# Recurrences of two mixers: chunks taken in pairs, lower grams moved ahead, no products with the zero state, filler products before the first merges

## What is computed

```python
lower = jnp.where(strict, jnp.einsum('bhncd,bhnsd->bhncs', kb, k) * decay, 0.0)
rhs = jnp.concatenate([v * beta[..., None], kb * jnp.exp(g)[..., None]], axis=-1)
sol = lax.linalg.triangular_solve(jnp.eye(C) + lower, rhs, left_side=True, lower=True, unit_diagonal=True)
...
def step(S, inp):
    qc, kc, uc, wc, gc, ac = inp
    v_new = uc - jnp.einsum('bhck,bhkv->bhcv', wc, S)
    o = jnp.einsum('bhck,bhkv->bhcv', qc * jnp.exp(gc)[..., None], S) + jnp.einsum('bhcs,bhsv->bhcv', ac, v_new)
    S = S * jnp.exp(g_last)[..., None, None] + jnp.einsum(...)
    return S, o
```

## Time and profile before

| | us |
|---|---|
| timed runs: median (lowest to highest, 3 runs) | 3484.34 (3483.23 to 3485.39) |
| profiled execution, its own time | 3478.72 |
| its span, first to last instruction | 3476.9 |
| TensorE busy | 3358.7 |
| recurrences' core, layer 0: 649.34 to 753.96 | 104.62 |
| recurrences' core, layer 1: 1802.64 to 1906.95 | 104.31 |

### The profile page before, as it was taken

The page is one execution under the profiler, slowest core; times in us unless marked ns, Lnnn a source line. Parts: engine busy times, 40 slices in busy tenths (PEclk is TensorE's granted clock), DMA queues, the critical chain, the costliest instruction groups (busy, mean ns, idle before and its releaser), DMA issues.

```text
span 3476.9 us, 47334 instructions
## 1 busy us (share of the span) xinstructions
PE 3358.7 (97%) x16932; PEld 2760.2 (79%) x16932; DVE 1424.3 (41%) x2739; ACT 1267.1 (36%) x1976; POOL 1675.9 (48%) x2052
## 2 busy tenths in 40 slices
PE   7999998899999999999989999999899999999999
PEld 6888776788888888887668888878667888888887
DVE  5431598855221322148786522123663110441100
ACT  4222436534222322234563422232533332433321
POOL 6765542006665566655400466645304555435554
PEclk9999999799999999999979999999999999999999
DMA  5443321003443344333100344332102222212222
GB/s 186 145 145 109 109 91 56 13 19 133 145 144 110 127 145 145 121 103 98 61 25 1 109 145 145 127 104 82 58 1 91 97 97 97 85 61 97 97 97 97
DMA packets 104225, 340.51 MB, mean 98 GB/s; under 512 B 12144, under 2 KB 17936, under 8 KB 103968
## 3 DMA queue, kind: packets, MB, share of 16 engines
q1 hardware_dynamic: 87824, 283.08, 24.6%
q10 hardware_dynamic: 16272, 55.65, 4.8%
HBM read 330.78 MB, written 2.65 MB: 96 GB/s over the span
## 4 chain that ended last, share of the span: by engine, by line
issue 38%; POOL 33%; PE 27%; DVE 1%; POOLq 0%; ACT 0%; DVEq 0%
POOL w_lo L721 33%; PE ps L2313 7%; PE ps L2314 7%; PE ps L2315 7%; PE ps L3094 1%; PE ps L2336 0%; PE ps L3073 0%; PE ps L2337 0%; PE ps L2341 0%; PE ps L3082 0%; PE ps L3184 0%; DVE stat L2214 0%; DVE sq L2207 0%; PE ps L3190 0%; PE ps L3074 0%
## 5 line engine op out<-in xcount | busy, mean ns | idle before, releaser
L721 POOL TENSOR_TENSOR w_lo<-w_raw,w_hi 128x256 fp32r<-128x256 f32 x2040 | 1669.2, 850 | 1783.3 <-ACT w_hi L764 1776.1
L2313 PE MATMUL ps<-h_hi,w_hi 128*128 128x512 f32 x2608 | 1019.9, 391 | 0.9 <-ACT mem L981 0.9
L2315 PE MATMUL ps<-h_hi,w_lo 128*128 128x512 f32 x2608 | 1015.7, 389 | 0.0
L2314 PE MATMUL ps<-h_lo,w_hi 128*128 128x512 f32 x2608 | 1015.6, 389 | 0.0
L764 ACT ACTIVATE w_hi<-w_raw 128x1024 fp32r<-128x1024 f32 x510 | 538.2, 1057 | 927.2 <-DMA w_raw<-in_tiles 927.0
L2313 PEld LDWEIGHTS ps<-h_hi,w_hi 128*128 128x128 f32 x2608 | 490.0, 188 | 113.3 <-issue 6.4
L2315 PEld LDWEIGHTS ps<-h_hi,w_lo 128*128 128x128 f32 x2608 | 490.0, 188 | 102.9
L2314 PEld LDWEIGHTS ps<-h_lo,w_hi 128*128 128x128 f32 x2608 | 490.0, 188 | 100.3
L2314 PE MATMUL ps<-a_lo,w_hi 128*128 (+1 forms) x1120 | 435.8, 389 | 0.0
L2313 PE MATMUL ps<-a_hi,w_hi 128*128 (+1 forms) x1056 | 410.8, 389 | 0.0
L2315 PE MATMUL ps<-a_hi,w_lo 128*128 (+1 forms) x1056 | 410.8, 389 | 0.0
(11 more groups left out here) (477 smaller groups left out, 3589.4 us busy)
## 6 DMA issues: line engine op xcount, KB each, us to landing
w_raw<-in_tiles SPq DMA_DIRECT2D x510, 512.0 KB, 3.3
ada_raw<-in_ada_tiles ACTq DMA_DIRECT2D x96, 512.0 KB, 3.3
mem<-mem SPq DMA_DIRECT2D x80, 64.0 KB, 2.1
x<-in_x_t SPq DMA_DIRECT2D x2, 1024.0 KB, 6.6
sq<-in_cond ACTq DMA_DIRECT2D x4, 512.0 KB, 4.2
mem<-gates SPq DMA_DIRECT2D x8, 256.0 KB, 3.9
consts<-in_consts SPq DMA_DIRECT2D x1, 1280.0 KB, 12.8
core_mem<-gates SPq DMA_DIRECT2D x8, 128.0 KB, 2.9
```

The lines of the kernel that those rows point to most:

```text
L721: ins = nc.gpsimd.tensor_tensor(w_lo[:, s, part], w_raw[:, s, part], w_hi[:, s, part].bitcast(F32), ALU.subtract)
L2313: nc.tensor.matmul(bank, wh, hi, start=first, stop=False, skip_group_check=True)
L2314: nc.tensor.matmul(bank, wh, lo, start=False, stop=False, skip_group_check=True)
L2315: return nc.tensor.matmul(bank, wl, hi, start=False, stop=last, skip_group_check=True)
```

## The change

- The chunks are taken in two pairs, (0, 1) and (2, 3). VectorE substitutes both chunks of a pair at once (16 heads in one operation where there were 8), and the mask of the small blocks is multiplied once per pair. The merge levels alternate between the even and the odd chunk; then the even chunk, then the odd one, is run through right sides, writes and outputs.
- Level 4 masks its first product on VectorE (`mask_products`, 64 columns a head) instead of masking the lower matrix beforehand (`lower_corners`, removed), makes one product instead of two, and VectorE transposes the merged inverse (blocks of 32) for the other. ScalarE's copy of level 4 goes.
- All lower grams are made early: chunk 1 after the first turn, chunk 2 after the sixth, chunk 3 after the last, each behind a wait for PSUM to be taken. Their units are separate.
- The first chunk leaves out the products with the zero state, and `next_state(1)` writes without the old state. The state has two slots in turn.
- Eight products of 128 columns with no use stand ahead of the first level-4 products.
- ScalarE takes the decays of chunks 2 and 3 after the turns instead of before them; the silu of the gate moves there too. Output grams lie in other units, outputs in one PSUM bank.
- The constants sel_pair, sel_head and the level mask are no longer loaded.

The diff, cut to its core (ScalarE, then VectorE, then TensorE):

```diff
-                act.wait_ge(S["spread_taken"], 3 * l + 3)
-                decays(2)
-                decays(3).then_inc(S["eg_ready"], 1)
-                load_silu()
-                act.wait_ge(S["rwkv_ready"], l + 1)
-                nc.scalar.activation(mem[:, 37:39, :], core_mem[:, G_CONV + 4:G_CONV + 6, :], ACT.Silu).then_inc(S["conv_act_v"], 1)
                 for u in (2, 3, 4, 5, 0, 1):
                     turn_out(mem[:, u, :])
                 for c, u in enumerate((45, 6)):
                     turn_out_scaled(mem[:, u, :], c, ST_DELTA)
+                load_silu()
+                act.wait_ge(S["rwkv_ready"], l + 1)
+                nc.scalar.activation(mem[:, 37:39, :], core_mem[:, G_CONV + 4:G_CONV + 6, :], ACT.Silu).then_inc(S["conv_act_v"], 1)
+                nc.scalar.activation(mem[:, U_Z:U_Z + 2, :], mem[:, U_Z:U_Z + 2, :], ACT.Silu)
                 for c, u in enumerate((26, 19)):
                     turn_out_scaled(mem[:, u, :], c, ST_BETA)
-                spread_diagonal(l, 0)
-                for n in range(TB + 1):
-                    core_step(l, n)
+                act.wait_ge(S["spread_taken"], 3 * l + 3)
+                decays(2)
+                decays(3).then_inc(S["eg_ready"], 1)
+                core(l)
...
+                def mask_products(n):
+
+                    own_pair = ODD_QUARTER.unsqueeze(1).unsqueeze(3).to_broadcast([P, 4, 4, 16])
+                    for g in range(2):
+                        dve.wait_ge(S["t1_ready"], merge_turn(TB * l + n, 4, g) + 1)
+                        out, src = (ap.rearrange("p (h q c) -> p h q c", h=4, q=4) for ap in (t1_of(n, g), ps[:, merge_bank(n, g), 0:HALF]))
+                        V.tensor_tensor(out, src, own_pair, ALU.mult).then_inc(S["t1_out"], 1)
+
+                def merge16(n):
+
+                    for g in range(2):
+                        inv, inv_t = inv_units(n)[:, g, :], inv_t_units(n)[:, g, :]
+                        dve.wait_ge(S["dx_ready"], merge_turn(TB * l + n, 4, g) + 1)
+                        link(V.tensor_tensor(evens(inv, 4), evens(inv, 4), compact(ps[:, merge_bank(n, g), half[0]], 4), ALU.add))
+                        V.transpose(inv_t, inv).then_inc(S["merged16"], 1)
...
+                substitute(range(15, 0, -1))
+                dve.wait_ge(S["turned"], 10 * (l + 1))
+                dve.wait_ge(S["vf_moved"], 16)
+                spread_inverses(l, 0)
+                fresh_rows()
+                mask_products(0)
+                dve.wait_ge(S["eg_ready"], 4 * l + 4)
+                take_grams(l, 2)
+                mask_products(1)
+                take_grams(l, 3)
+                merge16(0)
+                merge16(1)
+                small_blocks(l, 2)
+                small_blocks(l, 3)
+                later = slice(P, T)
+                V.tensor_tensor(mem[:, 37:39, later], mem[:, U_QG:U_QG + 2, later], mem[:, 41:43, later], ALU.mult)
+                V.scalar_tensor_tensor(mem[:, 24:26, later], mem[:, 39:41, later], -1.0, mem[:, 41:43, later], ALU.mult, ALU.mult).then_inc(S["gdn_ready"], 1)
+                dve.wait_ge(S["gdn_ready"], l + 1)
+                take_a_grams(0, range(4))
+                substitute(range(15, 8, -1))
+                next_state(1)
+                take_a_grams(1, range(4))
+                substitute(range(8, 4, -1))
+                next_state(2)
+                substitute(range(4, 0, -1))
+                spread_inverses(l, 2)
+                mask_products(2)
+                mask_products(3)
+                merge16(2)
+                take_a_grams(2, range(4))
+                merge16(3)
+                take_a_grams(3, (0, 1))
+                next_state(3)
+                take_a_grams(3, (2, 3))
...
+                    if at == 1:
+                        pe.wait_ge(S["gram_taken"], 2 * TB * l + 2)
+                        lower_grams(l, 1)
+                    if at == 6:
+                        pe.wait_ge(S["gram_taken"], 2 * TB * l + 4)
+                        lower_grams(l, 2)
...
+                def inverse_products(n, lev):
+
+                    b = TB * l + n
...
+                    for g in range(2):
+                        pe.wait_ge(S["t1_out"], merge_turn(b, lev, g) + 1)
+                        bank = merge_bank(n, g)
+                        inv_t = lambda h: inv_t_units(n)[:, g, blk(h)]
+                        t1 = lambda h: t1_of(n, g)[:, HD * h:HD * h + HD]
+                        if lev < 6:
+                            first = 0 if lev == 4 else 32
+                            for h in range(4):
+                                ins = nc.tensor.matmul(ps[0:P - first, bank, HD * h:HD * h + HD], inv_t(h)[:, first:P], t1(h), start=True, stop=True)
+                        if lev > 4:
+                            for h in range(4):
+                                out = compact(ps[0:HD, bank, HALF + HD * h:HALF + HD * h + HD], lev)
+                                ins = nc.tensor.matmul(out, t1(h), odds(inv_t(h), lev), start=True, stop=True)
+                        ins.then_inc(S["dx_ready"], 1)
...
+                pe.wait_ge(S["turned_out"], seen["turn"])
+                lower_grams(l, 3)
+                for _ in range(8):
+                    nc.tensor.matmul(ps[:, 5, 0:P], const("ident"), const("ones"), start=True, stop=True)
+                for even in (0, 2):
+                    odd, n = even + 1, even + 1
+                    if even:
+                        pe.wait_ge(S["a_gram_out"], 4 * (TB * l + 2))
+                    lower_products(even, 4)
+                    lower_products(odd, 4)
+                    inverse_products(even, 4)
+                    inverse_products(odd, 4)
+                    if even:
+                        pe.wait_ge(S["s_out"], (TB - 1) * l + 2)
+                        pe.wait_ge(S["y_out"], TB * l + even)
+                    else:
+                        pe.wait_ge(S["gram_taken"], 2 * TB * (l + 1))
+                    a_grams(even, (0, 1))
+                    lower_products(even, 5)
+                    lower_products(odd, 5)
+                    inverse_products(even, 5)
+                    inverse_products(odd, 5)
+                    lower_products(even, 6)
+                    inverse_products(even, 6)
+                    right_sides(n)
+                    lower_products(odd, 6)
+                    writes(n)
+                    a_grams(odd, (0,))
+                    inverse_products(odd, 6)
+                    state_products(n)
+                    outputs(n)
+                    pe.wait_ge(S["merged64"], 2 * (TB * l + odd) + 2)
+                    a_grams(odd, (1,))
+                    right_sides(n + 1)
+                    writes(n + 1)
+                    state_products(n + 1)
+                    outputs(n + 1)
```

More of the change, by code:

```diff
@@ L598, in _ @@
         def _(sp):
-            first, last = 2 * P, CONST_AT["eps"]
+            first, last, small = 2 * P, CONST_AT["sel_pair"], CONST_AT["eps"]
             half = KD // 2
@@ new lines, in core @@
+                for even in (0, 2):
+                    odd, n = even + 1, even + 1
+                    spread_diagonal(l, even)
+                    spread_diagonal(l, odd)
+                    products_out(even, 5)
+                    products_out(odd, 5)
+                    merge32(even)
+                    merge32(odd)
+                    products_out(even, 6)
+                    merge64(even)
+                    right_out(n)
+                    products_out(odd, 6)
+                    writes_out(n)
+                    merge64(odd)
+                    outputs_out(n)
+                    if n + 1 == TB:
+                        for k in range(4):
+                            nc.scalar.activation(attended_hi[:, k, :], mem[:, U_Y + k, :], ACT.Copy).then_inc(S["h_hi_ready"], 1)
+                    right_out(n + 1)
+                    writes_out(n + 1)
+                    outputs_out(n + 1)
@@ L2703, in recurrences @@
                     turn(src, turn_bank(n))
-                pe.wait_ge(S["turned_out"], seen["turn"])
-                for n in range(TB + 1):
-                    core_step(l, n)
+                core(l)
                 post(l)
@@ L2790, in a_grams, with right_sides @@
+                def a_grams(n, kinds):
+                    for kind in kinds:
+                        pairs = ((kt, ap), (kt, rt)) if kind == 0 else ((nb, rt), (kg, qg))
+                        grams([a_banks(n, 2 * kind + hh) for hh in range(2)], "a_gram_ready", pairs, n)
+                def right_sides(n):
+                    b, last = TB * l + n, n - 1
+                    pe.wait_ge(S["merged64"], 2 * b)
+                    pe.wait_ge(S["a_gram_out"], 4 * b if n == 1 else 4 * b - 2)
                     if n > 1:
-                        grams((6, 7), "a_gram_ready", ((nb, rt), (kg, qg)), last)
@@ new lines, in outputs @@
+                def outputs(n):
+                    b, last = TB * l + n, n - 1
```

(7 more changed lines are left out.)

391 lines of the change are left out of this document (147 added, 244 removed).

## The result

| | before | after |
|---|---|---|
| median of the timed runs, us | 3483.85 (3482.38 to 3486.93, 8 runs) | 3497.97 (3493.27 to 3500.58, 8 runs) |
| ratio | | 1.0034, 95% interval 1.0025 to 1.0043 |
| profiled execution, us | 3478.72 | 3500.58 |
| recurrences' core, layer 0, us | 104.62 | 103.79 |
| recurrences' core, layer 1, us | 104.31 | 106.49 |

The change makes the kernel 14.1 us slower, by the medians.

What follows compares the result with a forecast made beforehand. TensorE's queue was taken to bound the kernel. In layer 0, 654.1 + 40.7 + 6.6 + 42.9 + 8.7 = 753.0 against 753.96; with layer 1 and hand-overs, about -1 us: 3483.3, range 3466 to 3500.

Steps and rivals of the forecast that it cites:

- the clock fell twice: Stated sign that the prediction is wrong: TensorE's granted clock dropping twice; no further 0.50 was expected in the first pair.
- the doubled steps: VectorE's 15 substitution steps on two chunks at once, put at 14.8 us; costing more was a sign of being wrong.
- The first merge: Start of the first pair's level 4: 654.1 us, bounds 653.3 and 657, against 649.3 before; 4.8 us lost.
- Fillers and first pair: Eight unused products raise the clock before level 4; first pair then takes 40.7 us, level 4 of it 7.2.
- rival 4: Fillers ahead of level 4 run slow and end after operands are ready: start 657, +5 us, 3489; chance 0.12.
- Rival 3: Clock falls in the first pair, or stays low beyond the second pair's output grams: +12.7 us, 3497; chance 0.26.
- The gap: Between the pairs TensorE idles 6.6 us, waiting for VectorE's state, four substitution steps and spread, 9.1 us together.
- Rivals 1 and 2: Clock stays up across the gap: 3466, chance 0.12; or no gap between the pairs: 3453, chance 0.05.
- Level 4 of the second pair: Behind the idle time it runs at half clock, with some output grams: 8.7 us lost a layer.
- Outputs with state: Chunk outputs including the state's products, put at 2.5 us from the old kernel's durations.
- The hand-overs around writes of chunks 2 and 4: TensorE to ScalarE and back, 0.7 us each, no longer covered by other work; 0.5 us a layer added.
- The spared work: Chunk 1's products with the zero state left out: 2.1 us less TensorE work a layer.

Runs made afterwards that it cites:

- no_fillers: The changed kernel without the eight unused products ahead of the first level-4 products: 3512.46 us.
- steps_early: The changed kernel with VectorE's late substitution steps and the second pair's spread moved ahead of the two state updates: 3475.25 us.
- gap_filled: The changed kernel with 22 unused products behind chunk 2's outputs, in TensorE's idle time between the pairs: 3483.30 us.
- after_state_split: The changed kernel with the state products of chunk 2's and 4's outputs moved into the hand-overs, each group with its own PSUM bank: 3487.13 us.
- after_holes_filled: The changed kernel with three unused products in each of the two hand-overs of chunks 2 and 4: 3488.53 us.
- zero_cost_back: steps_early with eight unused products where the zero-state products were left out, four ahead of chunk 1's right sides, four ahead of its outputs: 3481.56 us.
- state_split: steps_early with the state products of chunk 2's and 4's outputs moved into the hand-overs, each group with its own PSUM bank: 3463.44 us.
- gap_half: The changed kernel with two of the four late substitution steps moved ahead of chunk 2's state update: 3491.98 us.

## Why the prediction was wrong

It said 3483.3, no change that can be told, and the kernel is 14.1 us slower; 3497.97 lies inside the range, near its upper end. Two of its own signs of being wrong came true: the clock fell twice in layer 0's core, and the doubled steps took 14.87 us for 14.8, the second without weight. Step by step:

- **The first merge** was to start 4.8 us later. It started 7.6 later (656.92 for 649.34), of which 2.56 come from the start of the kernel and 0.94 from the attention, which the change does not touch. 4.1 are left, and in layer 1 5.4, counted from the same place in the attention: right within its bounds. The substitution took 14.9 us (638.97 to 653.84).
- **Fillers and first pair** (rivals 3 and 4): level 4 at 7.2 us, in layer 0 no half clock from its first product to chunk 2, in layer 1 0.9 us of it at level 4's start. Right; no_fillers shows that the eight products are why. They ended after the operands were ready, as rival 4 says, but by 0.9 and 1.5 us and inside the bounds of the start. Rival 3's time, 3497, is met by chance: its mechanism, half clock in the first pair, is not there, and the second pair stayed low beyond its output grams by 0.7 and 1.8 us only.
- **The gap**: 5.75 us for 6.6, in layer 1 5.27. With outputs(2), which were longer, 9.5 for 9.1. Right, and steps_early and gap_filled show its whole price, 22.7 us of which 14.7 are the clock. Rivals 1 and 2 fall.
- **Level 4 of the second pair**: 18.2 us of work at half, 9.1 lost, for 8.7; in layer 1 19.3 and 9.7. Right. The Trainium skill (TensorE: Matmul & The Clock Gate, HAM oscillation) has this as bursts that start at half clock after a wait. The traces agree for 4.06, 4.40 and 5.75 us. Behind 2.60 and 2.42 us the clock stayed up; the waits of the page's own case are longer than these two.
- **Outputs with state**: 2.5 us. This term was mis-sized. They take 3.49 at the upper clock. I had taken the durations of the old order, in which four state products stand in a row, each with its bank, and the change alternates them with 64-row products in one bank (which of the two matters is not shown). In chunk 2 the surplus hid in the gap (after_state_split); chunks 3 and 4 pay 2 us a layer, 4 in all.
- **The hand-overs around writes of chunks 2 and 4**: "I add 0.5 a layer". This is the step that failed. I had each at 0.7 and its length is right, but I priced the idle time alone. after_holes_filled puts their clock at 9.4 us: half clock in chunk 2's state products, on the way to the gap, and behind chunk 4 in the output tiles. I looked for the clock only up to the core's last product, and took 2.60 us borne once as a pardon for all shorter waits. The Trainium skill (TensorE: Matmul & The Clock Gate, A second HAM failure mode) names short idle times between groups of products as a second way to an oscillating clock; after_holes_filled agrees, with 9.4 us for eight waits of 0.69.
- **The sum**: -1 as forecast, + 9.4 + 4 = 12.4, against 14.1 measured. The two corrections come from different kernels and may share some clock (after_state_split, which has chunk 4's part of both, took back 10.8), so the 1.7 left over is not assigned. By the two profiles the loss is not the same in both layers, though I had worked out one and taken it twice: from the same place in the attention to a place in the output tiles behind every stretch of half clock, layer 0 loses 3.2 us and layer 1 12.2. Layer 1 has the two stretches at and behind chunk 4, 17.06 us in all and 8.4 lost, and layer 0 none.
- **The spared work**: 2.1 us a layer for the zero state holds in the new order (zero_cost_back) and has the other sign in the old one. The start-up constants are worth nothing that can be measured, as counted.

Left open: why the clock behind chunk 4 stays up in some executions and falls in others (layer 1 and not layer 0 in the profile after), why the same wait of 1.38 us was borne three times in ten, and what makes the first 44 us 1.6 to 3.2 us longer in about half of the profiles.

## What to carry to other kernels

An idle time of the bounding engine has two prices, its length and the clock of what stands behind it, and here the second was the larger: ask for every wait that an edit leaves with nothing queued beside it, even one of 0.7 us, what runs after it, also past the end of the stage. Work that is removed from in front of a wait is not a gain but a longer wait; so move the late engine's steps first (VectorE had 9.5 us of idle time ahead of the two state updates, and moving eight steps and the spread there turned 14 us lost into 7 gained). And when an edit changes the order of products, take durations from rows that have the new order, not from those that have the same products.

## What was not expected of the hardware

- Leaving out eight products (2.1 us of TensorE's work a layer) made the kernel before 3.8 us slower, and eight products without use brought it back (3487.09, 3482.47).
- A state product (128 rows out) between 64-row products cost about 0.5 us, in a row 0.25: outputs(2) 3.49 us, and 1.46 without the four, which then filled 0.96 us of idle time (0.69 and 0.69 us became 0.24 and 0.18).
- Behind the same thin products the clock stayed at 1.00 in four of four places where no wait followed, and fell in seven of ten where 1.37 or 1.38 us of wait did (13.65 us of 0.50 in state_split). In gap_half single runs of one kernel lay 27 us apart (3478.67 to 3505.24).
